# A decoder layer's router stage: x put into the accumulators by identity products, counts in fp32r, h written turned in halves, gates behind the selection, the first gather in four banks

## The reference, cut to what matters

```python
def grouped_moe(h, router_w, router_b, w_gate, w_up, w_down):
    probs = softmax(h @ router_w + router_b)             # 16 experts in 4 groups of 4
    group_score = sum of the two best probs of a group
    best = argmax(group_score)                           # one group for each token
    top_p, top_i = top_k(probs within the best group, 2)
    gates = one_hot(top_i) * top_p / sum(top_p)
    for e in range(16):
        a = silu(h @ w_gate[e]) * (h @ w_up[e])          # 1024 -> 512
        out = out + gates[..., e:e + 1] * (a @ w_down[e])
    return out

x = x + grouped_moe(rms_norm(x, norm_ffn), ...)
```

## Time and profile before

| | us |
|---|---|
| median of 3 runs | 622.98 (622.82 to 623.06) |
| profiled execution, device time | 622.19 |
| its span, first to last instruction | 620.4 |
| TensorE busy | 598.5 (96%), mean granted clock 0.984 |
| VectorE busy | 275.1 (44%) |
| ScalarE busy | 238.0 (38%) |
| DMA | 164.09 MB, mean 265 GB/s |

### The profile page before, as it was taken

One profiled execution on the slowest core, in us unless ns is written; L12 is line 12 of the kernel. 1 busy time (PEld: TensorE's weight loads), 2 busy tenths in 40 slices (PEclk: granted clock), 3 DMA queues, 4 the chain that ended last, 5 costly groups with the idle time before them and its releaser, 6 DMA issues.

```text
span 620.4 us, 7541 instructions
## 1 busy us (share of the span) xinstructions
PE 598.5 (96%) x2962; PEld 397.9 (64%) x2962; DVE 275.1 (44%) x414; ACT 238.0 (38%) x318; POOL 19.1 (3%) x13
## 2 busy tenths in 40 slices
PE   5999999999999999999999999999999999999995
PEld 4887888877876778888888788444434434443332
DVE  3734686854577653886755545111112112110002
ACT  5643573654484554733463552311111111111111
POOL 0100000050020000000101000000000000000000
PEclk9999999999999999999999985999999999999999
DMA  9964566854452336655521699599999999999931
GB/s 331 365 215 137 174 234 208 300 203 137 148 159 100 102 111 230 203 195 158 190 68 32 256 422 409 221 422 421 421 422 421 420 421 421 422 420 419 420 153 68
DMA packets 49055, 164.09 MB, mean 265 GB/s; under 512 B 4377, under 2 KB 9179, under 8 KB 36732
## 3 DMA queue, kind: packets, MB, share of 16 engines
q1 hardware_dynamic: 44432, 158.81, 66.7%
q10 hardware_dynamic: 4588, 4.80, 2.3%
HBM read 162.53 MB, written 2.64 MB: 266 GB/s over the span
## 4 chain that ended last, share of the span: by engine, by line
PE 90%; ACT 3%; DVE 3%; issue 1%; DMA 1%; DVEq 1%; SPq 0%; POOL 0%; ACTq 0%
PE ps L1837 18%; PE ps L1427 15%; PE ps L1419 14%; PE ps L1420 14%; PE ps L1852 9%; PE ps L1400 5%; PE ps L1781 4%; PE ps L1872 3%; PE ps L1563 1%; DMA w_raw<-in_w_in 1%; PE ps L1589 1%; PE ps L1724 1%; PE ps L1770 1%; ACT w_hi L504 1%; PE ps L1701 1%
## 5 line engine op out<-in xcount | busy, mean ns | idle before, releaser
L874 DVE TENSOR_TENSOR w_lo<-w_raw,w_hi 128x2048 fp32r<-128x2048 f32 (+2 forms) x54 | 118.5, 2211 | 56.2 <-ACT w_hi L504 55.6
L1419 PE MATMUL ps<-w_hi,act_hi 128*128 128x512 f32 (+1 forms) x304 | 118.7, 392 | 1.6 <-ACT w_hi L504 1.6
L1420 PE MATMUL ps<-w_hi,act_lo 128*128 128x512 f32 (+1 forms) x304 | 116.3, 384 | 0.0
L504 ACT ACTIVATE w_hi<-w_raw 128x2048 fp32r<-128x2048 f32 (+2 forms) x54 | 99.1, 1856 | 27.6 <-PE ps L1427 26.1
L1837 PE MATMUL ps<-e_raw,xg 128*64 128x512 f32 x368 | 82.4, 596 | 0.0
L1427 PE MATMUL ps<-w_lo,act_hi 128*128 128x512 f32 (+1 forms) x304 | 74.3, 386 | 0.0
L1419 PEld LDWEIGHTS ps<-w_hi,act_hi 128*128 128x128 f32 x304 | 57.1, 188 | 14.1 <-issue 3.3
L1420 PEld LDWEIGHTS ps<-w_hi,act_lo 128*128 128x128 f32 x304 | 57.2, 188 | 10.6
L1427 PEld LDWEIGHTS ps<-w_lo,act_hi 128*128 128x128 f32 x304 | 55.6, 188 | 11.5 <-issue 0.7
L1837 PEld LDWEIGHTS ps<-e_raw,xg 128*64 128x64 f32 x368 | 25.1, 137 | 45.6 <-issue 44.0
L813 ACT ACTIVATE gu<-ps,rs_slot 128x512 f32<-128x512 f32 x16 | 11.0, 687 | 111.7 <-PE ps L1837 111.7
(11 more groups left out here) (299 smaller groups left out, 721.7 us busy)
## 6 DMA issues: line engine op xcount, KB each, us to landing
w_raw<-in_w_in SPq DMA_DIRECT2D x32, 1024.0 KB, 5.5
e_raw<-in_w_expert_down SPq DMA_DIRECT2D x26, 1024.0 KB, 14.8
e_raw<-in_w_expert_gate SPq DMA_DIRECT2D x23, 1024.0 KB, 14.2
e_raw<-in_w_expert_up SPq DMA_DIRECT2D x23, 1024.0 KB, 15.9
w_raw<-in_w_expert_gate SPq DMA_DIRECT2D x9, 1024.0 KB, 11.3
w_raw<-in_w_expert_up SPq DMA_DIRECT2D x9, 1024.0 KB, 13.4
w_raw<-in_w_expert_down SPq DMA_DIRECT2D x6, 1024.0 KB, 14.0
w_raw<-in_w_xkv SPq DMA_DIRECT2D x4, 1024.0 KB, 5.6
```

What stands on the lines that cost most here:

```text
L504: A(bview(w_hi, b, blocks[b].shape), bview(w_raw, b, blocks[b].shape), ACT.Copy).then_inc(hi_done, 1)
L874: V.tensor_tensor(bview(w_lo, b, sh), bview(w_raw, b, sh), f32(bview(w_hi, b, sh)), ALU.subtract).then_inc(lo_done, 1)
L1419: MM(o, xh[:, t0 + k, i * P:(i + 1) * P], wh[:, k], start=first and k == 0, stop=False)
L1420: MM(o, xl[:, t0 + k, i * P:(i + 1) * P], wh[:, k], start=False, stop=False)
```

## The change

- `h_full` is written by VectorE in the turned order at once, in halves; ScalarE makes `h_hi` and VectorE `h_lo` in halves too, the first half behind the first half of the residual, the second around the choice. `h_turn` goes.
- The products of zeros go. Four fp32 products of the identity with `x_res`, 512 columns each, put x into banks 4 to 7, all before the counts. One more such product into bank 0 follows (`keep_busy(1)`), and two behind the counts (`keep_busy(2)`).
- The counts are four fp32r products, on copies of `before` and `ones` in fp32r (`count_w`) and a choice written in fp32r (`chosen_r`).
- The selection tiles come first; the gates are computed by VectorE behind the first gather's copies, and `slot_gates` of group 0 stands in expert 0 between the two halves of its gate and up products.
- The first gather goes through banks 0 to 3 by turns.
- At the end two copies on ScalarE and two on VectorE take the place of four additions.

```diff
-                    sp.wait_ge(s["out_ready"], 2 * i + half + 1)
+                    sp.wait_ge(s["out_ready" if half else "out_by_act"], i + 1)
...
+            def h_hi_half(n):
+                act.wait_ge(s["h_full_done"], n + 1)
+                A(h_half(h_hi, n), h_half(h_full, n), ACT.Copy).then_inc(s["h_hi_done"], 1)
+
             for i in range(NT):
                 x2_square(0, i)
+            h_hi_half(0)
             x2_out(0)
             x2_out(1)
...
-            act.wait_ge(s["h_full_done"], 2)
-            h_turned(0)
+            h_hi_half(1)
             act.wait_ge(s["router_max_taken"], 1)
             A(prob[:], prob[:], ACT.Exp).then_inc(s["router_exp_done"], 1)
-            h_turned(1)
-            act.drain()
-            A(h_hi[:], h_turn[:], ACT.Copy).then_inc(s["h_hi_done"], 1)
...
+            for i in range(NT):
+                act.wait_ge(s["scattered"], rounds * (2 * NE) + i)
+                A(x_res[:, i, 0:COLS], ps[:, 4 + 2 * i, :], ACT.Copy).then_inc(s["out_by_act"], 1)
...
-                return V.tensor_tensor(h_full[:, i, cs], x_res[:, i, cs], g_ffn_row[:, cs], ALU.mult)
+                natural = lambda v: v.rearrange("q (p t) -> q p t", t=KD)
+                return V.tensor_tensor(h_half(h_full, n)[:, i].rearrange("q t p -> q p t"), natural(x_res[:, i, cs]),
+                                       natural(g_ffn_row[:, cs]), ALU.mult)
...
+            def h_lo_half(n):
+                dve.wait_ge(s["h_hi_done"], n + 1)
+                V.tensor_tensor(h_half(h_lo, n), h_half(h_full, n), f32(h_half(h_hi, n)), ALU.subtract).then_inc(s["h_lo_done"], 1)
+
+            h_lo_half(0)
             dve.wait_ge(mm_done, first_block[C_XO + 2])
...
+            def residual(i):
+                for half in range(2):
+                    MM(ps[:, 4 + 2 * i + half, :], ident[:], x_res[:, i, half * COLS:(half + 1) * COLS], start=True, stop=False,
+                       skip_group_check=True)
+
+            def keep_busy(count):
+                for k in range(count):
+                    MM(ps[:, 0, :], ident[:], x_res[:, 0, 0:COLS], start=True, stop=True)
+
+            for i in range(NT):
+                residual(i)
+            keep_busy(1)
+
+            pe.wait_ge(s["count_w_ready"], 1)
             pe.wait_ge(s["chosen"], 1)
...
+            MM(ps[:, 1, 0:NT * NE], count_w[:, 0], chosen_r[:].rearrange("p i e -> p (i e)"), start=True, stop=False, skip_group_check=True)
+            MM(ps[:, 1, NE:2 * NE], count_w[:, 1], chosen_r[:, 0], start=False, stop=True, skip_group_check=True)
+            MM(ps[:, 1, 2 * NE:3 * NE], count_w[:, 1], chosen_r[:, 0], start=True, stop=False, skip_group_check=True)
+            MM(ps[:, 1, 2 * NE:3 * NE], count_w[:, 1], chosen_r[:, 1], start=False, stop=True,
+               skip_group_check=True).then_inc(s["places_done"], 1)
+            keep_busy(2)
             pe.drain().then_inc(s["scattered"], 1)
...
-                    if t == 1:
-                        pe.wait_ge(s["slot_gates_moved"], r * NG + 1)
-                    if t >= 2 and t % 2:
-                        pe.wait_ge(s["odd_moved"], r * ODD + t // 2)
-                    elif t >= 2:
-                        pe.wait_ge(s["even_moved"], r * (KD // 2) + t // 2)
-                    gather_tile(0, t, t % 2, first)
+                    if t >= 4:
+                        pe.wait_ge(s["odd_moved"], r * ODD + (t // 2 - 1)) if t % 2 else pe.wait_ge(
+                            s["even_moved"], r * (KD // 2) + (t // 2 - 1))
+                    gather_tile(0, t, t % 4, first)
...
                     gate_up(r, e, 0)
+                    if e == 0:
+                        slot_gates(r, 0)
...
-            slot_gates(0, 0)
             first_gather(0, first=True)
```

More of the change, by code:

```diff
@@ L228, in build_program @@
         h_full = sb("h_full", [P, NT, D])
-        h_hi, h_lo = sb("h_hi", [P, NT, D], f32r), sb("h_lo", [P, NT, D], f32r)
-        h_turn = at("h_turn", xg_at + 8192, [P, NT, D])
+        h_hi = sb("h_hi", [P, NT, D], f32r)
         sel = sb("sel", [P, NT, EPG, P], f32r)
@@ L239, in build_program @@
         y_hi, y_lo = sb("y_hi", [P, COLS], f32r), sb("y_lo", [P, COLS], f32r)
+        h_lo = sb("h_lo", [P, NT, D], f32r)
         route = sb("route", [P, 1024])
@@ L1198, in _ @@
             act_lo_part("o", range(2), oT_lo, oT_hi)
-            V.memset(zeros, 0.0).then_inc(s["zeros_written"], 1)
+            V.tensor_copy(count_w[:, 0], before)
+            V.tensor_copy(count_w[:, 1], ones).then_inc(s["count_w_ready"], 1)
             residual_add(C_XO, 0, 1.0)
@@ L1365, in expert_round @@
                 y_lo_part(r, NE - 1)
-            dve.wait_ge(s["h_hi_done"], 1)
-            for i in range(NT):
-                ins = V.tensor_tensor(h_lo[:, i, :], h_turn[:, i, :], f32(h_hi[:, i, :]), ALU.subtract)
-            ins.then_inc(s["h_lo_done"], 1)
             def first_gather_out(r):
@@ L1373, in first_gather_out @@
                     gather_out(r, 0, t)
-            slot_gates(0, 0)
             first_gather_out(0)
+            V.tensor_tensor(v84(topw), v84(r2), one_group, ALU.mult)
+            dve.drain()
+            V.reduce_sum(rsum, v2(topw), AX.X)
+            dve.drain()
+            V.reciprocal(rrec, rsum)
+            dve.drain()
+            V.tensor_tensor(v2(gates), v2(topw), two(rrec, NE), ALU.mult)
+            dve.drain()
+            V.tensor_copy(gates_split[:, :, 0], v2(gates))
+            dve.drain()
+            V.tensor_tensor(gates_split[:, :, 1], v2(gates), f32(gates_split[:, :, 0]), ALU.subtract)
+            dve.drain()
+            gates_of(0)
             dve.wait_ge(s["rounds_ready"], 1)
@@ L1388, in _ @@
                 dve.wait_ge(s["scattered"], rounds * (2 * NE) + i)
-                for half in range(2):
-                    x_ = x_res[:, i, half * COLS:(half + 1) * COLS]
-                    V.tensor_tensor(x_, ps[:, 4 + 2 * i + half, :], x_, ALU.add).then_inc(s["out_ready"], 1)
+                V.tensor_copy(x_res[:, i, COLS:2 * COLS], ps[:, 5 + 2 * i, :]).then_inc(s["out_ready"], 1)
         @block.tensor
@@ L1743, in _ @@
             ins.then_inc(s["router_logits_done"], 1)
-            def clear_banks(banks):
-                for b in banks:
-                    for k in range(4):
-                        MM(ps[:, b, k * P:(k + 1) * P], zeros, zeros, start=k == 0, stop=False, skip_group_check=True)
-            pe.wait_ge(s["zeros_written"], 1)
-            clear_banks(range(4, 6))
-            pe.wait_ge(s["chosen"], 1)
-            ch = chosen.rearrange("p (i e) -> p i e", i=NT)
-            MM(ps[:, 1, 0:NE], before, ch[:, 0], start=True, stop=True)
@@ L1756, in _ @@
-            MM(ps[:, 1, NE:2 * NE], before, ch[:, 1], start=True, stop=False)
-            MM(ps[:, 1, NE:2 * NE], ones, ch[:, 0], start=False, stop=True)
-            MM(ps[:, 1, 2 * NE:3 * NE], ones, ch[:, 0], start=True, stop=False)
-            MM(ps[:, 1, 2 * NE:3 * NE], ones, ch[:, 1], start=False, stop=True).then_inc(s["places_done"], 1)
-            clear_banks(range(6, 8))
+            def residual(i):
+                for half in range(2):
+                    MM(ps[:, 4 + 2 * i + half, :], ident[:], x_res[:, i, half * COLS:(half + 1) * COLS], start=True, stop=False,
+                       skip_group_check=True)
@@ L1807, in turn_selection @@
                     pe.wait_ge(s["selT_moved"], r * (2 * NG) + (2 * g + 1))
+                elif not half:
+                    pe.wait_ge(s["slot_gates_moved"], r * NG + (g + 1))
                 for e in (2 * half, 2 * half + 1):
@@ L1829, in gate_up @@
                     else:
[L1830 removed]
+                        pe.wait_ge(s["even_moved"], r * (KD // 2) + (4 if half else 3))
                         pe.wait_ge(s["odd_moved"], r * ODD + tiles // 2)
```

63 lines of the change are left out of this document (27 added, 36 removed).

## The result

The changed kernel takes 619.47 us, median of five runs (619.00 to 619.58), beside 622.82 us (622.06 to 623.06) for the kernel before on the same chip: a ratio of 0.9948, 95% interval 0.9933 to 0.9962. In a later round of runs it took 619.16 us, ratio 0.9929 (0.9911 to 0.9946). Predicted were 619.9 us, range 617.0 to 622.2. Its profiled execution took 619.0 us with a span of 617.2 us, against 622.19 and 620.4 us.

What follows compares the result with a forecast made beforehand. The prediction took the router stage's chain through VectorE and TensorE as the bound. First expert 4.2 us earlier, less 1.1 us paid back, gave 3.1 us: 622.98 - 3.1 = 619.9 us, range 617.0 to 622.2.

Steps and rivals of the forecast that it cites:

- What bounds the kernel: Router stage, a chain through VectorE and TensorE: a microsecond saved ahead of the first expert's products is one at the end.
- h halves: VectorE's strided h writes ahead of the router: 1.2 us each, 0.15 us passed on, 2.34 us of h_lo off the chain.
- Rival (c): Strided h write is dear: at 2.8 us each the kernel takes 624.5 us; slower from 2.5 us; chance 0.05.
- Identity products and the clock: TensorE ahead of the counts: clock back 4.5 us into the products, which end at 377.2; counts wait 1.9 us.
- rival (b): Identity products don't bring TensorE's clock back, as the zeros didn't; first expert at 391.4, 625.5 us; chance 0.08.
- Rival (a): Clock costs less: identity products end by 375.3 and counts start at once; 618.6 us, down to 617.1; chance 0.20.
- (d): Clock returns late, in the last of the identity products or in the keep-busy ones: 621 to 623 us; chance 0.07.
- Gates behind the selection: Selection ready 2.0 us after the counts; gate products return in expert 0 for 1.1 us, with 1.8 us of cover.
- Gather in four banks: First gather: 0.63 us a tile, more banks saving little; 5.0 us instead of 5.9, lower bound 4.2.
- entry into the loop: From gather's end to the first expert's products: 0.9 us instead of 1.0, bounds 0.5 and 1.0.
- The end: Two copies on each of two engines replace four additions; the store is limited by DMA: gain 0, bound 0.3 us.
- The total: First expert 4.2 us earlier, 1.1 us paid back, 3.1 us saved from 622.98: 619.9 us; chance 0.60 for 619.1 to 620.9.

Runs made afterwards that it cites:

- zeros_back: Changed kernel with the kernel before's products of zeros and its four additions at the end in place of the seven identity products: 618.65 us, ratio 0.9930.
- split22: Changed kernel with two identity products ahead of the counts, two behind, no keep-busy products, h_lo's second half ahead of the logits wait: 618.34 us, ratio 0.9934.
- fill1: Changed kernel with one more 512-column identity product in the 0.71 us gap ahead of the router's second half: 616.1 us, ratio 0.9907.
- zero_stationary: Changed kernel with a block of zeros in place of the identity in all seven 512-column products, x left out of the result: 617.93 us, ratio 0.9930.
- cols128: Changed kernel with each of the seven 512-column identity products cut into four of 128 columns, on real operands: 618.55 us, ratio 0.9927.
- split22_fill: Changed kernel with the edits of `split22` and `fill1` together: 620.7 us, ratio 0.9956.
- two_banks: Changed kernel with its first gather back in two banks by turns, with the waits that brings: 620.71 us, ratio 0.9962.
- fill1_early: Changed kernel with the extra product of `fill1` and h_lo's second half ahead of VectorE's wait for the logits: 617.67 us, ratio 0.9904.
- no_keep: Changed kernel without its three keep-busy products, one ahead of the counts and two behind: 620.19 us, ratio 0.9944.

## Why the prediction held, step by step

**What bounds the kernel** was right. Of the 5.47 us that the stage lost, 1.14 us came back in expert 0 and 4.3 us went through to the end. The waits of the changed kernel from 386 us on (engine, tile and line, what it waited for: total, times, longest) show no transfer for TensorE:

```profile
PE ps L1890 <- DVE y_lo L1343: 2.6, 2, 1.7
...
PE ps L1855 <- DVE xg L1338: 0.6, 1, 0.6
```

These are the last scatter's wait of the earlier trace rows, again 2.6 us, and the entry into the first expert.

**h halves.** Predicted 1.2 us for a strided write and 0.15 us passed on; measured 1.03 (two in 2.06) to 1.08 us and nothing: the router's first products start 6.28 us behind the residual in both kernels (358.07 to 364.35 before, 359.15 to 365.43 after). The surcharge is 0.34 to 0.39 us for 512 elements, under the 0.52 us of ScalarE's strided read the earlier trace rows. Rival (c) is out: it turned at 2.5 us. What the Trainium skill (Advanced Engine Details and Errata, Memory Cachelines) says of accesses to separate lines, as the prediction named it, agrees in its direction.

**Not in the prediction: 0.8 us more up to the logits.** The router's second half went from 2.67 to 3.49 us and begins a little later against its first. The clock fell 3.6 us behind the router's first products, 4.5 us behind them before, so all of the second half lay at 1.2 GHz. The change isn't shown to be the cause: `zeros_back` and `split22` have its code up to the logits, and there the clock fell 4.3 and 4.4 us behind and the second half took 2.84 and 2.75 us. Over the eleven profiles without a product in the gap the fall lies 3.5 to 4.5 us behind the first products. `fill1` shows the price: 1.96 us where the clock stays up.

**Identity products and the clock.** Predicted: clock back 4.5 us into them, end 6.7 us after their start, counts held for 1.9 us. Measured from their start at 372.24: back after about 3.7 us, end after 6.2, where the second count product begins (378.45; the record of the first, 378.02 with 0.58 us, overlaps the last product): the counts are held for 1.4 us behind the choice at 377.06. Choice to counts read took 1.91 us where 2.5 was predicted. The mechanism was right and its duration a little too long; the 4.5 us chosen between 3 and never lay 0.8 us too high. The reason given against rival (b), real operands and 512 columns, was wrong: neither matters (6.83 us down in `zero_stationary` and `cols128`). What the kernels differ in is that the work isn't broken off, which `zeros_back` and `split22` bear out in the executions that were profiled. Counting the return from the products' start was the weak part of the term: the clock came back 6.8 us behind its fall in `split22_fill` too, where the counts, two products, a gap of 0.23 us and the gather's start fill that time, and the kernel before's first stretch of zeros ended at 374.1, 5.2 us behind the fall. Why its clock stayed down as long as 17.1 us isn't shown. Rival (a) needed the clock back within 0.8 us and didn't come; (d) didn't either.

**Gates behind the selection.** Predicted 2.1 us from the counts' read to the gather, measured 2.01 (378.97 to 380.98). The insertion into expert 0 cost 1.14 us where 1.1 was predicted. The gate chain was ready at 387.14, TensorE came for it at 389.17: 2.0 us of cover where 1.8 was predicted.

**Gather in four banks: the term that was mis-sized.** The step "its four weight loads, two in 0.30 us, nearly fill that, so more banks save little there" failed. A tile took 0.47 us, not 0.63, so the gather took 4.0 us, not 5.0, below the lower bound of 4.2. `two_banks` shows that the banks did it. Doubling the 0.30 us of two loads to 0.60 for four was the slip: loads overlap, and the second starts 0.12 us behind the first, so that four in a row need 0.47 us, which is what the tile now takes. The entry into the loop took 0.59 us instead of 0.9, within the bounds. The two together are the 1.3 us by which the stage beat its forecast (5.5 against 4.2); the shorter stay of the counts (0.6) and the dearer router half (0.8) nearly cancel.

**The end.** Predicted gain 0: the last scatter's products to the end of the span took 5.15 us against 5.24. The copies are done sooner, the store goes on at the same rate:

```profile
612.02 1.08 ACT L846 ACTIVATE x_res<-ps 128x512 f32<-128x512 f32 x2 [1.61 <-PE ps L1890]
612.02 1.29 DVE L1402 COPY x_res<-ps 128x512 f32<-128x512 f32 x2 [0.83 <-PE ps L1890]
...
615.00:615.50 0.50, 0.00 (x0) 0.00 (x0) 0.00 (x0) 0.00 (x0) 0.00 (x0) 0.50 1.03 393
```

The four additions of 2.48 us became 1.29 us on two engines side by side, and the DMA engines are as full as before.

**The total.** By the stage, 622.98 - 4.3 = 618.7 us was to be expected; the two medians are 619.47 and 619.16. So the forecast of 619.9 lay nearer than its terms did, by luck: the stage and expert 0 gained 1.2 us more than predicted, and 0.5 to 0.8 us of that is not in the medians. One execution's profile can't place so small a remainder. Two things in the record are larger. The profiled execution of the kernel before is one with much time at the low clock, a mean of 0.984, where 34 of its 51 other runs beside the experiments had 0.987 to 0.990; so 25.62 us may be more than its stage takes as a rule. And the work ahead of the router moves: the first products of the whole program ran at half the clock in the changed kernel's profile, at the full one before, with the same code. By the end of that block it is 1.06 us behind (the next begins at 16.17 us against 15.11), which is the 1.08 us of the section on the result.

```profile
11.57 0.63 PE L1431 MATMUL ps<-w_hi,act_lo 128*128 128x512 f32 x1
```

```profile
11.67 0.39 PE L1420 MATMUL ps<-w_hi,act_lo 128*128 128x512 f32 x1
```

The first line is of the changed kernel, the second of the one before. The Trainium skill (TensorE: Matmul & The Clock Gate, Part 1) says that the number of slow products at a kernel's start varies from run to run; the traces agree, 0.63 against 0.39 us for the same product.

## What to carry to other kernels

Price a repeated tile by what paces it: look whether the loads really fill it or whether the copy out of its bank does, before calling further banks worthless. Ahead of a dense stretch it was worth more here to keep TensorE's clock from falling, with one wide product in a gap, than to bring it back with filler in front of work that somebody waits for. Look at the mean clock of the other runs before taking one profile's clock for the kernel's. And read every moved step twice, once where it leaves and once where it arrives: of the 1.7 us that the gates took from the router stage, 1.15 came back in the first expert.

## What the runs showed of the hardware

- The clock came back 3.4 to 4.2 us into unbroken products, 6.8 us behind its fall in all eight profiles, at operands of zeros or of real data and at 128 or 512 columns; in the profiled executions of `zeros_back` and `split22`, 3.76 us of products followed by a break didn't bring it back (13.65 us down).
- One product of 512 columns (0.89 us at the full clock) in a gap of 0.71 us was enough to keep 2.4 GHz through the router's narrow products, in three profiles of three (`fill1`, `split22_fill`, `fill1_early`); without it the clock fell in eleven of eleven. The clock also held through 2.18 us of idleness (`no_keep`) and fell in one of 3.99 us (`split22_fill`).
- A VectorE write of 512 fp32 elements with a stride of 512 bytes took 1.03 to 1.08 us, a plain one 0.69.
- Four banks in place of two took a gather tile of four products from 0.61 to 0.47 us (`two_banks`).
- The first large products of the program took 0.63 us in some executions and 0.39 us in others, about 1 us of the whole time.
